# Softmax division moved from VectorE to GpSimd in a four-attention decoder trunk, with a new order of first loads and weight sums

## What is computed

```
sc = q_block @ k.T * scale + bias_and_mask
p  = softmax(sc)                  # exp(sc - max) / sum(exp(sc - max)); in SWA a sink logit is in the sum
o  = p @ v
```

## Time and profile before

| | us |
|---|---|
| three timed runs | 1070.09, 1070.62, 1070.86 |
| their median | 1070.62 |
| the profiled execution | 1067.56 |
| span that its profile covers | 1065.7 |

### The profile page before, as it was taken

One profiled execution on the slowest core, in us unless ns is written; L12 is line 12 of the kernel. 1 busy time (PEld: TensorE's weight loads), 2 busy tenths in 40 slices (PEclk: granted clock), 3 DMA queues, 4 the chain that ended last, 5 costly groups with the idle time before them and its releaser, 6 DMA issues.

```text
span 1065.7 us, 13549 instructions
## 1 busy us (share of the span) xinstructions
PE 982.3 (92%) x5440; PEld 632.7 (59%) x5440; DVE 415.4 (39%) x1126; ACT 230.7 (22%) x576; POOL 151.0 (14%) x126
## 2 busy tenths in 40 slices
PE   6999999999999999999779999989998999998976
PEld 4888588864556566665434666446454666665642
DVE  4734812381263332222153329258036233222215
ACT  3213710271120000000021227247012000000002
POOL 5562203001000111111001001000101011111100
PEclk9999999999999999999989999999999999999999
DMA  9529602186349999999997220034444799999996
GB/s 338 194 92 219 168 1 102 57 331 228 128 171 342 418 421 419 420 418 419 408 383 262 79 79 1 18 130 182 162 159 174 300 419 419 419 421 418 419 400 260
DMA packets 64129, 277.01 MB, mean 260 GB/s; under 512 B 12851, under 2 KB 17443, under 8 KB 39994
## 3 DMA queue, kind: packets, MB, share of 16 engines
q1 hardware_dynamic: 53808, 257.48, 62.6%
q0 software_dynamic: 10256, 18.64, 4.9%
HBM read 261.94 MB, written 30.44 MB: 274 GB/s over the span
## 4 chain that ended last, share of the span: by engine, by line
PE 67%; DMA 21%; DVE 5%; issue 4%; SPq 2%; POOL 1%; ACT 0%; POOLq 0%; DVEq 0%
PE bank L919 14%; PE bank L1032 10%; PE bank L1155 10%; DMA K<-rows,small 9%; PE bank L968 6%; PE bank L1169 5%; PE bank L904 4%; DMA D<-in_moe_w_down 4%; PE bank L892 3%; DMA hnT<-in_moe_w_down 3%; PE bank L986 3%; PE bank L1002 2%; PE bank L1371 2%; PE bank L1066 1%; DMA expert_rows<-K,small 1%
## 5 line engine op out<-in xcount | busy, mean ns | idle before, releaser
L1169 PE MATMUL bank<-D,PT 128*64 128x512 f32 x416 | 102.2, 594 | 11.4 <-DMA D<-in_moe_w_down 11.4
L1937 DVE SCALAR_TENSOR_TENSOR PT<-bank,small,PT 128x256 f32<-128x256 f32 x32 | 15.5, 484 | 201.3 <-PE bank L1155 201.3
L1155 PE MATMUL bank<-W,PT 128*64 128x256 f32 x640 | 79.0, 388 | 12.1 <-DMA W<-in_moe_w_up 5.0
L1959 DVE SCALAR_TENSOR_TENSOR K<-K,small,bank 128x512 f32<-128x512 f32 x64 | 47.8, 747 | 92.0 <-PE bank L1169 91.8
L716 POOL DMA_INDIRECT expert_rows<-K,small x30 | 30.2, 1008 | 344.9 <-DVE K L1959 319.8
L1155 PE MATMUL bank<-W,cst 128*64 128x256 f32 x640 | 76.9, 379 | 0.0
L1506 ACT ACTIVATE P<-P,nm 128x128 f32<-128x128 f32 (+5 forms) x128 | 68.3, 536 | 23.5 <-DVE nm L1731 23.1
L968 PE MATMUL bank<-K,Q 128*128 128x256 f32 (+3 forms) x256 | 70.4, 416 | 2.2 <-DVE nm L1731 1.0
L1155 PEld LDWEIGHTS bank<-W,PT 128*64 128x64 f32 x640 | 52.2, 139 | 31.8 <-issue 12.7
L1169 PEld LDWEIGHTS bank<-D,PT 128*64 128x64 f32 x416 | 36.2, 137 | 56.2 <-issue 47.1
L1546 ACT ACTIVATE PT<-bank 128x256 f32<-128x256 f32 x32 | 12.3, 384 | 261.7 <-PE bank L1161 245.4
(11 more groups left out here) (286 smaller groups left out, 1677.9 us busy)
## 6 DMA issues: line engine op xcount, KB each, us to landing
D<-in_moe_w_down SPq DMA_DIRECT2D x48, 1024.0 KB
W<-in_moe_w_gate SPq DMA_DIRECT2D x40, 1024.0 KB
W<-in_moe_w_up SPq DMA_DIRECT2D x36, 1024.0 KB
hnT<-in_moe_w_down SPq DMA_DIRECT2D x12, 1024.0 KB, 19.7
W<-in_e_w_in SPq DMA_DIRECT2D x5, 2048.0 KB
expert_rows<-K SPq DMA_DIRECT2D x2, 4096.0 KB, 36.0
V<-in_moe_w_gate SPq DMA_DIRECT2D x6, 1024.0 KB
Q<-in_moe_w_gate SPq DMA_DIRECT2D x6, 1024.0 KB
```

Of the source, the lines that this page charges most:

```text
L1155: last = nc.tensor.matmul(bank[b][at, 0:256], XT[k // 4][:, k % 4, at], w[:, 256 * k:256 * k + 256], start=(k == 0), stop=(k == KD - 1))
L1169: last = nc.tensor.matmul(bank[5 + half][at, :], hT[:, 128 * c + 64 * a:128 * c + 64 * a + 64], d[:, col:col + 512], start=(c == 0), stop= ...
L1959: nc.vector.scalar_tensor_tensor(rows[:, at], rows[:, at], own[:, p:p + 1], bank[5 + half][:, :], ALU.mult, ALU.add).then_inc(s_ye, 1)
```

## The change

1. Division: VectorE keeps only the reciprocal (`invert_sums`), which now raises a new semaphore s_rden. The four multiplies of each head move to GpSimd (`normalise(f)`, all 8 heads of an attention in one loop) and still raise s_nrm. The place in GpSimd's list: DIL behind sum_weights(2), FOX behind sum_weights(5), SWA behind the two copies L825 and L826, MLA behind the qrot DMA.
2. sum_weights(3) and sum_weights(4), before that ahead of and beside DIL, now stand behind all heads of DIL; the position rows for FOX are behind them.
3. The two copies of the rotary keys (L833) now stand behind all heads of SWA; the qrot DMA behind them.
4. Start: row chunks 2 and 3 are issued ahead of both halves of weight tile 0.
5. The semaphore of the latent root is dropped; that root counts in s_sqrt.

```diff
@@ SyncE
             for c in range(C):
-                if c == 2:
-                    load_first_half(0)
                 sp.dma_start(h[:, c, :], x[0, 128 * c:128 * c + 128, :]).then_inc(s_x[c], 16)
...
-                sp.wait_ge(s_sqrt, 8 * (lay + 1))
+                sp.wait_ge(s_sqrt, (8, 17)[lay])
...
-            load_first_half(1)
+            for half in range(2):
+                load_first_half(half)
             sp.dma_start(cst[:, C_MASKS:C_END], const_table[:, C_MASKS:C_END]).then_inc(s_masks, 16)
@@ GpSimd
+            def normalise(f):
+
+                for u in range(H):
+                    g = H * f + u
+                    pool.wait_ge(s_rden, g + 1)
+                    for i in range(4):
+                        b = 4 * g + i
+                        blk = P[:, u % 2, p_col(f, i):p_col(f, i) + LEN[f][i]]
+                        nc.gpsimd.tensor_scalar(blk, blk, rden[:, b % 8:b % 8 + 1], None, ALU.mult).then_inc(s_nrm, 1)
...
-            for n in (2, 3, 4):
-                sum_weights(n)
+            sum_weights(2)
+            normalise(DIL)
+            pool.wait_ge(s_nrm, 4 * H)
+            sum_weights(3)
+            sum_weights(4)
...
             sum_weights(5)
+            normalise(FOX)
             routing(0)
...
             nc.gpsimd.tensor_copy(uq[:, :, 112:128], uq[:, :, 64:80]).then_inc(s_perm, 1)
 
+            normalise(SWA)
+            pool.wait_ge(s_nrm, 4 * 3 * H)
             pool.wait_ge(s_ltV, C)
...
             pool.dma_start(qrot, const_qrot).then_inc(s_small, 16)
+            normalise(MLA)
             routing(1)
@@ ScalarE
-            nc.scalar.activation(rstd[:, :], ssq[:, :], ACT.Sqrt).then_inc(s_lrt, 1)
+            nc.scalar.activation(rstd[:, :], ssq[:, :], ACT.Sqrt).then_inc(s_sqrt, 1)
@@ VectorE
-                dve.wait_ge(s_sqrt, 4 * v + c + 1)
+                dve.wait_ge(s_sqrt, 4 * v + c + 1 + (v > 2))
...
-            def normalise(f, u):
+            def invert_sums(f, u):
 
                 g = H * f + u
                 dve.wait_ge(s_exp, 4 * g + 4)
                 sums = slice(4 * (g % 2), 4 * (g % 2) + 4)
-                then(nc.vector.reciprocal(rden[:, sums], den[:, sums]))
-                for i in range(4):
-                    b = 4 * (H * f + u) + i
-                    blk = P[:, u % 2, p_col(f, i):p_col(f, i) + LEN[f][i]]
-                    nc.vector.tensor_scalar(blk, blk, rden[:, b % 8:b % 8 + 1], None, ALU.mult).then_inc(s_nrm, 1)
+                nc.vector.reciprocal(rden[:, sums], den[:, sums]).then_inc(s_rden, 1)
...
-                        normalise(f, u + 2)
-                        normalise(f, u + 3)
+                        invert_sums(f, u + 2)
+                        invert_sums(f, u + 3)
...
-            dve.wait_ge(s_lrt, 1)
+            dve.wait_ge(s_sqrt, 13)
```

More of the change, by code:

```diff
@@ L382, in trunk @@
         s_lms = sem("latent_mean_square")
-        s_lrt = sem("latent_root")
+        s_rden = sem("sums_inverted")
         s_perm = sem("rotary_copies")
@@ L1759, in first_probs @@
                 masks(f, 1)
-                normalise(f, 0)
-                normalise(f, 1)
+                invert_sums(f, 0)
+                invert_sums(f, 1)
             def attention(f):
```

## The result

The changed kernel takes 1122.92 us (median of 4 runs, 1121.32 to 1125.59), the kernel before beside it 1070.36 us (4 runs, 1068.97 to 1070.86): 1.0495 of it, interval 1.0468 to 1.0521. It is 52.6 us slower, where 1.4 us were predicted, with a range of 1065 to 1088. The two profiled executions lie 56.1 us apart (1123.68 and 1067.56), because that of before was 2.8 us under its median and that of the changed kernel 0.8 over.

The account below looks back on a forecast made before the run. TensorE, 92% busy, was taken to bound the kernel, except VectorE in SWA. Causal attentions +4.8, MLA's head -3.2, SWA -0.2, the rest 0 gave +1.4 us on 1070.62: 1072.0, range 1065 to 1088.

Parts of the forecast that it names:

- the price of the moved step: GpSimd's time for a head's four multiplications, estimated from its copies: 1.85 us causal, 1.53 in SWA.
- X: Time in which GpSimd multiplies the four blocks of a causal head: 1.85 us forecast, range 1.3 to 3.2.
- the prediction's own formulas: Transposes' start per pair of heads from GpSimd's price: DIL +0.4, FOX +2.1, MLA +2.3, SWA -0.2 us.
- Rival D: GpSimd multiplies at the add's rate, X = 3.2: +23 us, 1094, idles possibly bringing the half clock; chance 0.16.
- X - 1.22: Delay of the transposes in each ordinary pair of a causal attention: +0.63 us.
- DIL's wait: TensorE's 1.89 us wait in DIL, beside GpSimd's sum_weights(4), goes when that sum moves; first pair -1.33 us.
- MLA's head: VectorE's copy no longer waits behind eight multiplications: idle 2.69 to 0.9 us, -1.75, clock stays up, -1.45; sum -3.2.
- The front: Row chunks ahead of the weights at the start: cost 0, bounds -0.8 to +1.5 us.
- The moved sums: sum_weights(3) and (4) behind DIL: first sum at 134.5 for about 142, the other near 151 for 166; no cost.
- qrot: Its DMA behind SWA's K copies lands 6.6 us after the last head, needed at 8.0: hidden by 0.7 us.
- The sinks copy in SWA: VectorE's copy stops meeting GpSimd's K copy (1.53 us for 0.16) but meets the multiplications: +0.2 us twice.
- the slope of the sum: Total change per us of X: 16 us, 12 in the causal attentions and 4 in SWA.

Follow-up runs that it names:

- filled kernel: Changed kernel plus two or three 512-column products that feed nothing, where TensorE waits for GpSimd: 1110.27 us, 1.0386 of before.
- kernel 7: Kernel before with the moves of rows, sums and SWA's K copies together, division left on VectorE: 1062.62 us, 0.9945 of before.
- 1 to 4: Changed kernel with, in turn: mixed GpSimd forms (1199.88 us), a quarter of the columns multiplied (1236.31), half of them (1279.92), extra products in TensorE's waits (1110.27).
- 9: Changed kernel with GpSimd's multiplication in the two-input form in all four attentions: 1081.31 us, 1.0122 of before.
- experiment 5: Kernel before with only row chunks 2 and 3 issued ahead of both halves of weight tile 0: 1.0001 of before.
- 6: Kernel before with only sum_weights(3) and (4) moved behind all of DIL, division on VectorE: 0.9982 of before.
- 10: Changed kernel with the division on GpSimd only in FOX, on VectorE elsewhere, all moves kept: 1.0114 of before.
- experiment 1: Changed kernel with another GpSimd form per attention: scalar from SBUF (DIL), constant (FOX), copy (SWA), two-input multiplication (MLA); 1199.88 us in one execution, routing changed.
- experiment 11: Changed kernel with each head's division shared, GpSimd blocks 0 and 2, VectorE blocks 1 and 3: 1074.23 us, 1.0050 of before.
- half kernel: Changed kernel with GpSimd multiplying only the first half of each block's columns: 1279.92 us, routing changed.

## Why the prediction was wrong

**The step that failed is the price of the moved step.** I bounded X by a one-input copy from below and a two-input add from above, 1.3 to 3.2, and chose near the copy because one input and one output were "as here". It is 4.24 (SWA 3.28 for 1.53). By the prediction's own formulas that makes DIL +9.9, FOX +11.7, MLA +11.9 and SWA +6.8: +40.3 where +4.6 stood. The upper bound was no bound: nothing said that an add with two inputs must be dearer than a multiplication by a scalar, and it is cheaper (2.31 ns a column against 2.49). "A cheap edge of D" at 3.2 should have been open above.

**The formulas left out the second head.** X - 1.22 counts the wait of the pair's first head. At full clock the second head's transposes stand 3.31 us after the first's (2.35 in SWA), and GpSimd does the heads in a row, so beyond X = 3.31 they wait too: 4.24 - 3.31 = 0.93 us for each of two ordinary pairs in three attentions, and 3.28 - 2.35 = 0.93 twice in SWA, 7.4 us. GpSimd is still idle between pairs then (8.50 us of work in a period of 12.95 in the filled kernel), but both heads of a pair wait for it. With it the formulas give +47.7; the filled kernel shows +47.85.

**The half clock was named and not priced.** Rival D said that idles of 2 to 4 us could bring it again, with 23 us for D in all. It cost 11.2 us more. 40.3 + 7.4 + 11.2 = 58.9, against 59.05 measured in the attentions. Of these the 11.2 is itself measured (changed less filled kernel); what tests the formulas is 47.7 for 47.85.

**What was right.** TensorE's order was read rightly: at X = 1.82 the four stages come out within 0.3 us each (for FOX and MLA that is closer than an unchanged kernel repeats itself). DIL's wait goes (-1.97 with the sums alone, 1.89 forecast). MLA's head gave -3.44, forecast -3.2, in these lines of the changed kernel:

```profile
746.41 1.88 PE L1404 MATMUL bank<-W,hnT 128*128 128x512 f32 x4
...
747.23 0.17 DVE L1757 RECIPROCAL rden<-den 128x4 f32<-128x4 f32 x1
...
749.25 3.67 PE L1404 MATMUL bank<-W,hnT 128*128 128x512 f32 x8 [0.95 <-ACT V L1515]
```

Idle 0.95 us for 0.9 forecast, and the full clock. The part of it that is clock (5.37 to 3.67 = 1.70, forecast 1.45) can't be given to the change for certain, since kernel 7 had it with the old idle. But all six kernels with the whole loop on GpSimd there (the changed one, 1 to 4 and 9) had an idle of 0.95 us and the full clock, and four of the five with 2.69 us (before, 5, 6, 10, not 7) had not. The 1.74 us less of idle are the change's. The front is worth 0 as said (experiment 5), the product that now needs the later half tile waited 1.18 us for it, and it started at 14.81, not at 14.93 as in the earlier trace rows. The moved sums are hidden: DIL to FOX takes 77.34 us in both kernels. qrot is hidden: it is asked for at 711.84, as TensorE starts at 712.06, and SWA to MLA still shows the whole gain.

**The sinks copy in SWA** was to lose 0.2 us twice beside GpSimd's multiplications. Timeline of the changed kernel:

```profile
681.69 6.58 POOL L786 TENSOR_SCALAR P<-P,rden 128x128 f32<-128x128 f32 x8 [9.05 <-DVE rden L1757]
...
686.28 0.22 DVE L1742 COPY P<-sinks 128x4 f32<-128x4 f32 x1
...
688.33 0.98 PE L1002 MATMUL bank<-cst,P 128*128 128x128 f32 x7 [0.78 <-POOL P L786]
```

It took 0.22 us, against the 1.53 beside the K copy and 0.16 alone. That is 0.06 lost and not 0.2.

**Rules beside the rows.** The copy runs near a column a nanosecond on GpSimd, the multiplication by a scalar at a third of that (experiment 1). The Trainium skill, "GPSIMD Engine Reference", section 4.1, calls one-input work on GpSimd "roughly line-rate". Experiment 1 agrees for the copy (256 columns in 401 ns) and not for the multiplication by a scalar (922 ns). The Trainium skill has in section 3.1 of the same page 769 ns for 512 elements in a tight loop, as the best case; no form of the multiplication comes near it (1560 and 1040 ns). The Trainium skill, "SBUF — State Buffer", "Who interferes with whom", would have a two-port VectorE operation that starts second wait for the whole GpSimd instruction. In experiment 11 VectorE's 512 columns, begun 0.27 us behind a GpSimd instruction of 1.38 us, took 0.73 us for 0.48: a delay, but not for the whole.

**Open.** When the clock halves was not settled. Behind waits of 2.93 us it did in eight of the nine ordinary or last pairs of the changed kernel's causal attentions (three of them for a part of the ten transposes), behind SWA's 2.41 not, behind the 2.30 of its last head for most of the seven transposes (1.76 us for 0.98), and behind FOX's second wait of 1.32 in the half kernel it did as well. Of single waits, 1.89 us in DIL of the kernel before left it up and 2.00 at MLA's head in experiment 11 did not; in FOX of experiment 1 it stayed up behind two waits of 2.59 and fell behind the third. So the length of the wait alone does not decide. What kept it up in kernel 7 behind 2.69 us isn't seen in any row either.

## What to carry to other kernels

Before a step moves to another engine, its price there has to come from a row of the same operation and form, not of one with as many inputs; where no such row exists, the range is open above, and the slope of the sum (here 16 us for each us) says what one measurement in isolation is worth. Ask of a producer that works for two consumers in a row at which price it bounds both, since the slope changes there. A moved step that lengthens the waits of the bounding engine can pay twice, once for the wait and once for the clock behind it; the moves that came with it gained 6 us without the division, 3.6 of them seen in the rows.

## What was not expected of the hardware

- GpSimd, float32, 128 partitions: multiplication by a scalar 2.49 ns a column and 0.28 us, whether the scalar is a constant (75 ns less) or comes from SBUF; the same product with the scalar as a broadcast second input 1.67 ns a column and 0.19 us; the copy 0.84 ns a column (401 and 293 ns for 256 and 128 columns). The two-input form is a third faster than the one-input form.
- Products that feed nothing, put in TensorE's waits, made the changed kernel some 12 us faster; the granted clock stayed at 1.00 in the windows of DIL and FOX.
- Behind the same wait of 2.69 us the granted clock fell in the kernels before, 5, 6 and 10 and stayed up in kernel 7.
- GpSimd and VectorE both multiplying: GpSimd's 128 columns took 0.95 us instead of 0.60 and VectorE's 512 columns 0.60 to 0.73 instead of 0.48, and VectorE's was not held for the whole of the GpSimd instruction beside it.
